# Four-round recurrent stage of a two-layer hybrid block: two PSUM banks per group of units, four array quadrants per product group

## The reference, cut to what matters

```python
def step(S, inp):
    r_t, w_t, k_t, v_t, kk_t, a_t = inp
    sa = jnp.einsum('bhij,bhj->bhi', S, kk_t)
    S = (S * w_t[:, :, None, :] - sa[..., None] * (kk_t * a_t)[:, :, None, :]
         + v_t[..., None] * k_t[:, :, None, :])
    return S, jnp.einsum('bhij,bhj->bhi', S, r_t)
...
s_ctx, y_c = wkv_scan(s0, rc, dec_c, kd_c, vc, kkc, a_c, rev)
_, y = wkv_scan(s_ctx, r, dec, kd, v, kk, a, rev)
ys.append(y)
```

## Time and profile before

| what | value |
|---|---|
| median of 3 runs | 3493.93 us (3493.92 to 3495.36) |
| the profiled execution's own time | 3495.4 us |
| its span, first to last instruction | 3493.6 us |
| PE busy | 3330.0 us (95%) |
| DVE busy | 1858.0 us (53%) |
| ACT busy | 1154.3 us (33%) |
| POOL busy | 412.4 us (12%) |
| mean granted TensorE clock | 0.985 of 2.4 GHz |

### The profile page before, as it was taken

The page is one execution under the profiler, slowest core; times in us unless marked ns, Lnnn a source line. Parts: engine busy times, 40 slices in busy tenths (PEclk is TensorE's granted clock), DMA queues, the critical chain, the costliest instruction groups (busy, mean ns, idle before and its releaser), DMA issues. The chain is left out here.

```text
span 3493.6 us, 68213 instructions
## 1 busy us (share of the span) xinstructions
PE 3330.0 (95%) x28698; PEld 2867.3 (82%) x28698; DVE 1858.0 (53%) x2801; ACT 1154.3 (33%) x1771; POOL 412.4 (12%) x280
## 2 busy tenths in 40 slices
PE   7999999999988899999999999999999978899999
PEld 5888888885668878888888888888895668789897
DVE  4552554665765555543554552554555765555353
ACT  3321222226652233321322331222226532234231
POOL 2000002004313211000002000002004233020000
PEclk9999999999999999999999999999999989999999
DMA  5222221440000012222221222221341000022222
GB/s 209 90 100 69 90 93 54 161 146 36 2 18 3 3 49 84 90 94 75 90 92 57 98 85 80 94 95 62 128 139 37 1 18 3 15 90 94 89 91 94
DMA packets 68294, 263.73 MB, mean 75 GB/s; under 512 B 7552, under 2 KB 8704, under 8 KB 67456
## 3 DMA queue, kind: packets, MB, share of 16 engines
q1 hardware_dynamic: 67664, 256.95, 21.9%
q10 hardware_dynamic: 432, 3.88, 0.3%
HBM read 258.70 MB, written 2.10 MB: 75 GB/s over the span
## 5 line engine op out<-in xcount | busy, mean ns | idle before, releaser
L240 PE MATMUL ps<-hn_hi,w_hi 128*128 128x512 f32 (+1 forms) x3520 | 864.3, 327 | 18.2 <-DVE hn_lo L457 5.9
L240 PE MATMUL ps<-hn_hi,w_lo 128*128 128x512 f32 (+1 forms) x3520 | 865.1, 327 | 0.0
L240 PE MATMUL ps<-hn_lo,w_hi 128*128 128x512 f32 (+1 forms) x3520 | 861.1, 326 | 0.0
L217 ACT ACTIVATE w_hi<-raw 128x1024 fp32r<-128x1024 f32 (+1 forms) x300 | 338.5, 1128 | 1376.8 <-PE ps L240 1224.1
L222 DVE TENSOR_TENSOR w_lo<-raw,w_hi 128x1024 fp32r<-128x1024 f32 (+1 forms) x300 | 396.8, 1323 | 470.8 <-ACT w_hi L217 463.4
L240 PEld LDWEIGHTS ps<-hn_hi,w_hi 128*128 128x128 f32 x3520 | 547.5, 190 | 82.7 <-issue 17.6
L240 PEld LDWEIGHTS ps<-hn_lo,w_hi 128*128 128x128 f32 x3520 | 548.2, 190 | 58.2
L240 PEld LDWEIGHTS ps<-hn_hi,w_lo 128*128 128x128 f32 x3520 | 545.0, 190 | 58.0
L240 PE MATMUL ps<-g_hi,w_hi 128*128 128x512 f32 (+1 forms) x1424 | 398.0, 347 | 6.1 <-DVE g_lo L894 6.1
L240 PE MATMUL ps<-g_lo,w_hi 128*128 128x512 f32 (+1 forms) x1424 | 403.6, 351 | 0.0
L240 PE MATMUL ps<-g_hi,w_lo 128*128 128x512 f32 (+1 forms) x1424 | 397.7, 347 | 0.0
(11 more groups left out here) (276 smaller groups left out, 4229.5 us busy)
## 6 DMA issues: line engine op xcount, KB each, us to landing
raw<-wgu SPq DMA_DIRECT2D x176, 512.0 KB, 3.5
w_mod_one<-wmod SPq DMA_DIRECT2D x100, 512.0 KB, 3.5
raw<-wdn SPq DMA_DIRECT2D x64, 704.0 KB, 4.0
raw<-win SPq DMA_DIRECT2D x44, 512.0 KB, 4.8
w_mod_two<-wmod SPq DMA_DIRECT2D x28, 512.0 KB, 3.7
w_mod_first<-wmod_first SPq DMA_DIRECT2D x4, 2048.0 KB, 22.5
raw<-wout SPq DMA_DIRECT2D x16, 512.0 KB, 3.5
h<-xT ACTq DMA_DIRECT2D x1, 3072.0 KB, 9.8
```

What stands on the lines that cost most here:

```text
L217: act.activation(w_hi[s][:, 0:kt, :].rearrange("p k n -> p (k n)"), raw[s][:, 0:kt * P], ACT.Copy).then_inc(hi_ready[s].sem, 1)
L240: mm = pe.matmul(out[:, o:o + b - a], w[:, k, :], m[:, k, a:b], start=(k == 0 and w is w_hi[s] and m is mov_hi), stop=(k == kt - 1 and w i ...
```

## The change: what it does, and the diff

1. The products that make X and its transpose XT from the block product now come in pairs: XT of a group goes to one bank from quadrants (0,0) and (1,1), X to another bank from quadrants (0,1) and (1,0) (`BANK_X`, `BANK_XT`). For that the block product of a level writes the other partition half (`hr(1 - b)`) and a group has its own two banks through all levels.
2. The masks of the levels are no longer put on the block product by DVE. POOL prepares masked copies of the block (`step_blocks`, 6 levels x 3 groups of 128x256 in a round, tiles `step_lo`), and DVE computes `eye - product` (`less_product`), so that the new X and XT are products and not differences. DVE copies X out (`inverse_out`) and ACT copies XT out (`transpose_out`).
3. Level 0 makes both X and XT by identity products (`first_step`, 16 products per group in place of 8).
4. TensorE's order: `low_rank` in two parts around level 1, the transposes one at a time between level products (`turn` 1 in level 2, 0 in level 3, 2 and 3 around level 5), all in slot 0 (banks 0 and 1); v is turned for the first direction of a head pair only. The MV products stand between the block products of level 3 or 4. ACT copies turns 0 and 1, DVE turns 2 and 3.
5. The chunk products go through the four quadrants in turn, and in the second layer the second half covers 4 of 6 token tiles (`OUT_TT`).
6. The chain begins with the second chunk's state (the first chunk's addend itself), keeps all states (`states`), has 10 steps, and puts outputs and score tiles at fixed places. The local outputs are added to `y_sum` before the chain's outputs (ACT copy for the first direction, DVE add for the second), and one DVE addition ends a round.

The core of the diff, TensorE and POOL (helpers first):

```diff
+            QUADRANTS = ((0, 0), (1, 1), (0, 1), (1, 0))
+            OUT_TT = nt // P
...
+            def step_blocks(pool, r, li, g):
+
+                d = ROUNDS[r][1]
+                mask = masks[:, d, 5:6, :] if li == 0 else masks[:, 1 - d, 5 + li:6 + li, :]
+                pool.wait_ge(wkv_masked.sem, wkv_masked.at(r * NTT + 2 * g + 2))
+                pool.tensor_tensor(step_lo[li][:, of_group(g), :], sc[:, of_group(g), 0, :], mask.broadcast_to([P, UG, CH]),
+                                   ALU.mult).then_inc(lo_masked.sem, 1)
...
+                    def first_step(r, g):
+
+                        pe.wait_ge(lo_masked.sem, lo_masked.at(blocks_until(r, 0, g)))
+                        if g >= 1:
+                            pe.wait_ge(wkv_masked.sem, wkv_masked.at(r * NTT + NTT - 2 + g))
+                        x, xt = in_bank(BANK_X[g]), in_bank(BANK_XT[g])
+                        for i, n in enumerate(units(g)):
+                            for b in range(2):
+                                pe.matmul(x[hr(b), i, :], step_lo[0][hr(b), n, :], K_["ident"][hr(b), hr(b)], start=True,
+                                          stop=True)
+                            for b in range(2):
+                                mm = pe.matmul(xt[hr(1 - b), i, :], K_["ident"][hr(b), hr(b)], step_lo[0][hr(b), n, :],
+                                               start=True, stop=True)
+                        mm.then_inc(lx_ready.sem, 1)
+
+                    def block_product(r, li, g, values=False):
+
+                        pe.wait_ge(x_ready.sem, x_ready.at(r * STEPS + GROUPS * (li - 1) + g + 1))
+                        pe.wait_ge(lo_masked.sem, lo_masked.at(blocks_until(r, li, g)))
+                        for i, n in enumerate(units(g)):
+                            for b in range(2):
+                                mm = pe.matmul(in_bank(BANK_X[g])[hr(1 - b), i, :], step_lo[li][hr(b), n, :], x_inv[hr(b), n, :],
+                                               start=True, stop=True)
+                                if values:
+                                    mv = pe.matmul(slots[0][hr(b), n * CH:(n + 1) * CH], sc[hr(b), n, 2, :],
+                                                   v_rw[hr(b), n // 2, hr(n % 2)], start=True, stop=True)
+                        mm.then_inc(lx_ready.sem, 1)
+                        if values and g == GROUPS - 1:
+                            mv.then_inc(mv_ready.sem, 1)
+
+                    def step_products(r, li, g):
+
+                        last = li == LEVELS - 1
+                        pe.wait_ge(t_ready.sem, t_ready.at(r * STEPS + GROUPS * (li - 1) + g + 1))
+                        if li >= 2:
+                            pe.wait_ge(xt_ready.sem, xt_ready.at(r * STEPS + GROUPS * (li - 2) + g + 1))
+                        for i, n in enumerate(units(g)):
+                            for b in (1, 0):
+                                mm = pe.matmul(in_bank(BANK_XT[g])[hr(b if last else 1 - b), i, :], lx[hr(1 - b), n, :],
+                                               xt_inv[hr(1 - b), n, :], start=True, stop=True)
+                            for b in (1, 0) if not last else ():
+                                mm = pe.matmul(in_bank(BANK_X[g])[hr(b), i, :], xt_inv[hr(1 - b), n, :], lx[hr(1 - b), n, :],
+                                               start=True, stop=True)
+                        mm.then_inc(step_ready.sem, 1)
...
+                        more = r + 1 < len(ROUNDS)
+                        for g in range(GROUPS):
+                            first_step(r, g)
+                        if r >= 1:
+                            pe.wait_ge(round_done.sem, round_done.at(r))
+                        else:
...
+                        if more:
+                            low_rank(r + 1, 0, slots[0])
+                        for g in range(GROUPS):
+                            block_product(r, 1, g)
+                        for g in range(GROUPS):
+                            step_products(r, 1, g)
+                        if more:
+                            pe.wait_ge(gate_tanh.sem, gate_tanh.at(2 * (r + 1) + 1))
+                            low_rank(r + 1, 1, slots[0])
+                        for g in range(GROUPS):
+                            block_product(r, 2, g)
+                        if more:
+                            pe.wait_ge(gate_tanh.sem, gate_tanh.at(2 * (r + 1) + 2))
+                        turn(r, 1)
+                        for g in range(GROUPS):
+                            step_products(r, 2, g)
...
+                        for li in (3, 4):
+                            values = li == 4 - d
+                            if values:
+                                free_of_turn(d)
                             for g in range(GROUPS):
...
+                                block_product(r, li, g, values)
+                            if li == 3 and d == 0:
+                                free_of_turn(1)
+                                turn(r, 0)
                             for g in range(GROUPS):
...
+                                step_products(r, li, g)
+                        for g in range(GROUPS):
+                            block_product(r, 5, g)
+                        pe.wait_ge(mv_copied.sem, mv_copied.at(r + 1))
+                        pe.wait_ge(features_end.sem, features_end.at(r + 1))
+                        turn(r, 2)
+                        for g in range(GROUPS):
+                            step_products(r, 5, g)
+                        pe.wait_ge(end_copied.sem, end_copied.at(2 * r + 1))
+                        turn(r, 3)
...
+                        for tt in range(NTT):
                             cc = slice(tt * CH, (tt + 1) * CH)
-                            for j in range(2):
-                                n = 2 * tt + j
-                                pe.matmul(ps[hr(j), 2 + b, cc], neg_w[hr(b), n, 0:64], b_nat[hr(b), tt, hr(j)],
+                            for j, b in QUADRANTS:
+                                pe.matmul(ps[hr(j), 2 + b, cc], neg_w[hr(b), 2 * tt + j, 0:64], b_nat[hr(b), tt, hr(j)],
                                           start=True, stop=True)
-                                pe.matmul(ps[hr(j), 4 + b, cc], b_nat[hr(b), tt, hr(j)], neg_w[hr(b), n, 64:128],
+                            for j, b in QUADRANTS:
+                                pe.matmul(ps[hr(j), 4 + b, cc], b_nat[hr(b), tt, hr(j)], neg_w[hr(b), 2 * tt + j, 64:128],
                                           start=True, stop=False)
+                            for j, b in QUADRANTS:
                                 mm = pe.matmul(ps[hr(j), 4 + b, cc], k_nat[hr(b), tt, hr(j)], v_rw[hr(b), tt, hr(j)],
...
+                        with_output = [i for i in range(NCH) if has_output(order[i])]
+                        OUTPUTS_AT = {i: [i] for i in range(5, NCH)}
+                        OUTPUTS_AT.update({2: [0], 3: [1, 2], 4: [3, 4]})
+                        SCORES_AT = {2: 0, 4: 1, 5: 2, 7: 3, 8: 4, 10: 5}
...
+                        addend(1)
+                        for i in range(1, NCH):
+                            if i >= 2:
+                                pe.wait_ge(state_ready.sem, state_ready.at(r * (NCH - 1) + i))
...
+                            if i == 2:
+                                pe.wait_ge(state_ready.sem, state_ready.at(r * (NCH - 1) + 1))
+                                pe.wait_ge(yloc_added.sem, yloc_added.at(r + 1))
                                 pe.wait_ge(reff_ready.sem, reff_ready.at(r + 1))
...
+                            for n in OUTPUTS_AT.get(i, ()):
+                                if n in with_output:
+                                    outputs(n)
...
+                            if more and i in SCORES_AT:
+                                score_tile(r + 1, SCORES_AT[i])
```

ScalarE's order in a round after the change, the removed lines left out:

```diff
+                        more = r + 1 < len(ROUNDS)
+                        if more:
+                            gate_tanhs(r + 1, 0)
+                            gate_decay(r + 1)
                         for g in range(GROUPS):
+                            transpose_out(r, 1, g)
+                        if more:
+                            gate_tanhs(r + 1, 1)
+                        transpose_out(r, 2, 0)
+                        copy_natural(r, 1)
+                        transpose_out(r, 2, 1)
+                        transpose_out(r, 2, 2)
+                        if more:
+                            gate_rate(r + 1)
+                        transpose_out(r, 3, 0)
...
```

VectorE, from the helpers to the copies of the turned tiles, and the addition of local outputs:

```diff
+                    def add_outputs(r):
+                        hp = ROUNDS[r][0]
+                        dve.wait_ge(y_ready.sem, y_ready.at(r + 1))
+                        dve.wait_ge(yloc_added.sem, yloc_added.at(r + 1))
+                        dve.tensor_tensor(y_sum[hp][:, Q], slots[0][:, Q], y_sum[hp][:, Q], ALU.add).then_inc(round_done.sem, 1)
+
+                    def inverse_out(r, li, g):
```

(36 more changed lines are left out.)

357 lines of the change are left out of this document (155 added, 202 removed).

## The result

The changed kernel takes 3439.7 us (median of four runs, 3436.6 to 3441.5) against 3493.9 (3491.9 to 3495.4): ratio 0.9842, 95% interval 0.9830 to 0.9855. That is 54 us gained where 129 were forecast. The direction was right and the size was wrong by more than a factor of two; the time lies between the forecast (3365) and the first rival (3452), inside the range.

A forecast was written before the change was run, and what follows sets the result against it. PE, busy 95% of the span, was taken as the bound. A middle round's terms sum to 41.0 us, 42.7 with the clock; layer gains of 60.3 and 68.7 us make 129, giving 3365 us, range 3335 to 3458.

The forecast's parts named there:

- first rival: All long runs on PE: a record is taken only every 28 ns, whatever quadrants and columns; 3452 us, chance 0.33.
- I take 14.6: 64-column products in four quadrants: 14.6 ns a record, half of 29.2; the likeliest case, chance 0.60.
- Levels 1 to 4: Middle levels of a round: 2.8 us of PE, put at 3.0 us each in place of 4.75.
- Chunk products: Two halves of 144 records at 14.6 ns: 4.2 us a round in place of 8.1.
- Level 0: First level: third group waits for POOL's thirteenth block, ready at T + 13.2; 5.2 us in rounds 2 to 4.
- Granted clock: PE's lower clock behind the wait before level 1: costs 1.7 us, kept for rounds 2 to 4.
- Chain: End of a round: head wait, score tiles, small products and gaps; 8.0 or 8.9 us by direction, mean 8.4.
- MV and turns: Between level products: MV's 48 records 0 us (1.4 without quadrant overlap), transposes 0.64 us each, 2.2 us.
- wait of 2.08 us before level 1: Kernel before: PE waits up to 2.08 us there, with level 0's 12 DVE operations in the way.
- third rival (slow blocks): POOL's blocks take 0.84 us, group 2 ready 2 to 3 us later in six rounds; 3385 us, chance 0.15.
- quadrants taking turns: Four-quadrant products writing the same partitions run one by one, 58 ns a record; 3652 us, chance 0.04.
- The rule of the Trainium skill with 25 ns: All matmuls: start-to-start time never below about 25 ns, if across quadrants too; about 3428 us.

The follow-up runs named there:

- micro: Changed kernel plus five long runs of small products on constants behind its last store; 64 columns in four quadrants: 3.61 us per 256 instructions, 28.2 ns a record.
- oldorder: Changed kernel with the chunk products put back in the order of the kernel before: 3458.6 us.
- pairs: Changed kernel with half of the levels' products left out and the other half made twice as wide (128 columns): 3406.7 us.
- border: Kernel before with one part of the change alone, chunk products through the four quadrants in turn: 3477.6 us.
- poolorder: Changed kernel with POOL's step blocks from round 2 on in the order in which PE wants them: 3411.2 us.
- split: Changed kernel with every chunk product cut into two of 32 columns, same columns and mathematics: 3510.2 us.
- lean3pairs: lean2 with other PSUM banks for W, state addends and local outputs, half of the levels' products left out, the others twice as wide: 3346.8 us.
- lean2: poolorder with level 0's four transposing products per group and quadrant merged, and chunk products that share weights made one of 128 columns: 3396.8 us.

## Why the prediction was wrong

The step that failed is "I take 14.6, since it is the same instruction pair in the same quadrant order as the score tiles", taken as a rate that lasts. As the spacing of two records it is right to the tenth. As the price of 144 or 288 of them in a row it needs 256 instructions every 1.87 us, and they come every 3.6 us (micro) to 4.1 us (in round 2 the packets of queue 8 start at 1100.97, 1105.00, 1108.91 and 1113.28). The trace of before could not show it: its only rows of that kind, the score tiles, are 16 records long and twice as wide, and its long runs were too slow to meet the limit. The forecast said itself that no row has 64-column records in all four quadrants; what it lacked was a price for that rate's not lasting. The first rival had the mean nearly right (28.2 ns) and the wrong mechanism, and my answers to it, row by row, were right: those 27 to 29 ns had causes of their own (micro and oldorder have the same rates without a pause).

Over the first layer the stage takes 199.1 us where 161.1 were forecast, 38 more. The 15 pauses are 21.4 us, counted from one weight load to the next. The lower clock lasts 27.2 us and costs at most half of that, 13.6, where 5.1 were forecast: 8.5. That leaves some 8 us that I did not settle.

By the prediction's own terms, for round 2 (51.6 us measured, 42.7 forecast):

- Levels 1 to 4, forecast 3.0 each: 3.6 to 5.5 us each here (with what stands between them), 2.65 where supply doesn't limit (pairs). Pauses of 0.8 and 1.7 us fall into them and one of 1.9 into level 5 (from one weight load to the next). The rate itself was right: the 96 step records of level 2 start within 1.41 us, 14.8 ns each.
- Chunk products, forecast 2 x 2.1 us: the first half 2.15 us, and the second 3.6 us with a pause of 1.6 in it. Before it was 8.1, so 2.4 of the forecast 3.9 us came, as border shows by itself.
- Level 0, forecast ready at T + 13.2 (T is the end of the chunk products) through 13 blocks of 0.68 us: POOL's 18 blocks take 12.35 us, 0.69 each, PE starts the third group at T + 13.5, DVE idles for 3.9 us ahead of it. Right.
- Granted clock, forecast 1.7 us: the timeline has the lower level for 6.8 us from 1078.8 in this round and for 10.2 in the next, at the end of the wait for POOL, so up to 3.4 and 5.1 us. Short by half or more; poolorder takes the wait away, and half of the lower level with it. The gate products and level 1 stand in that stretch.
- Chain, forecast 8.0 and 8.9 us: PE's last output starts at T + 7.9 and T + 8.7. Right. MV and turns: nothing to tell.

Pauses 6.0 and clock 1.7 are 7.7 of the missing 8.9 us; the rest lies in pieces of 0.7 us and less in levels 0 and 2 and around the transposes. POOL's row for this, and DVE's idle time behind it, kernel after:
```profile
1069.59 12.35 POOL L1791 TENSOR_TENSOR step_lo<-sc,masks 128x256 f32<-128x256 f32 x18 [5.27 <-DVE sc L2257]
...
1079.61 0.42 DVE L2279 TENSOR_TENSOR x_inv<-const,ps 128x256 f32<-128x256 f32 x1 [3.93 <-PE ps L2030]
```
```profile
1078.80:1085.60 6.80, 6.80 (x116) 4.99 (x110) 2.64 (x7) 1.84 (x2) 3.15 (x5) 0.50 0.01 2
```

One reading of the forecast was wrong without a price: it put PE's wait of 2.08 us before level 1 to DVE's operations. It ended with ACT's copy of MV, for which the program waits there; row of the kernel before:
```profile
1089.76 0.79 ACT L1809 ACTIVATE a_mv<-ps 128x768 f32<-128x768 f32 x1
```
The copy ends at 1090.55 and PE's weight loads go on at 1090.62. The profile says "issue" there too, so that word alone doesn't mean a page.

The third rival (slow blocks) and quadrants taking turns did not happen. The rule of the Trainium skill with 25 ns ("TensorE: Matmul & The Clock Gate") gave 3428 us and so came as near as the first rival (12 us off either way), but by chance: the records of 32 columns in micro start every 14.3 ns within a page (128 in 2.07 us, the last one's 0.25 taken off), four quadrants in turn, so its floor does not hold across quadrants.

## What to carry to other kernels

An engine that runs many short instructions can be limited by the fetching of them: count its instructions by 256, semaphore instructions too, and set 3.6 us or more against each page before a rate from a short burst is used for a long run. Pauses marked "issue" in the middle of a group, whole multiples of 256 instructions apart, are its sign; a wait marked "issue" ahead of a group can be a semaphore's. Then one wider instruction on shared weights helps where a better order of narrow ones no longer does. And a rate that no row shows for as long as it is needed is a risk that wants a price of its own in the range, even where its spacing is right.

## What the runs showed of the hardware

- TensorE's pages of 256 instructions, 3.47 to 3.75 us each in steady state with nothing else at work, about two held, the one in work and the next (border runs 216 chunk records at full rate and the kernel after 259, then they pause).
- In four quadrants a record starts every 14.6 ns with 64 columns and every 14.3 with 32: narrower products bring nothing. 128 columns 27.3 ns, 256 columns 54.4.
- The granted clock followed PE's idle time, but not the pauses' sum. In the kernel after (0.93) three of the four stretches at the lower level, 23.8 of 27.2 us, begin within 2 us of the end of a wait for POOL. split (0.86) has three of 13.7 us that begin among the pauses of its chunk products. lean3pairs, with almost no pauses, has 1.00, and lean2 has 0.99 with 16.4 us of them in its first stage:
```profile
1027.50:1202.60 175.10, 149.44 (x5163) 132.87 (x5164) 99.92 (x194) 73.81 (x160) 116.95 (x107) 0.99 0.03 10
```
- In micro the last 376 records of L2407 run at the lower level (row below) at 27.1 ns each and without a pause, no slower than the 27.1 to 29.3 ns a record that a page gives: the lower clock costs nothing there.
```profile
3545.00:3555.00 10.00, 10.00 (x376) 10.00 (x375) 0.00 (x0) 0.00 (x0) 0.00 (x0) 0.50 0.02 5
```
